# A two-block transformer on one core: closing a stage later, swapping two steps of a softmax pipeline on VectorE, and moving one weight load behind a wait

## What is computed

```python
q, k_cmp, v_cmp, ... = split(h @ w_in)            # 8 heads of 64, 2 key/value heads
for c in range(4):                                # 128 queries at a time
    s_c = q[c] @ k_cmp.T + head_bias(d_c)         # 31 compressed keys
    p_c = masked_softmax(s_c, d_c >= 0);  o_c = p_c @ v_cmp
    s_s = q[c] @ k_s.T + head_bias(d_s)           # selected keys
    p_s = masked_softmax(s_s, d_s >= 0);  o_s = p_s @ v_s
    s_w = q[c] @ k_w.T + head_bias(d_w)           # window of keys
    p_w = masked_softmax(s_w, m_w);       o_w = p_w @ v_w
    out[c] = g0 * o_c + g1 * o_s + g2 * o_w
mq, mk = silu(causal_conv(mq_mk) + b)             # for the mLSTM that follows
```

## Time and profile before

| | |
|---|---|
| median of 3 runs | 1873.73 us (1873.18 to 1878.88) |
| the profiled execution | 1878.88 us, span 1877.1 us |
| mean granted PE clock | 0.961 of full |
| busy over the span | PE 92%, PEld 66%, DVE 39%, ACT 32%, POOL 9% |
| chain that ended last | PE 69%, DMA 20%, DVE 5%, ACT 4% |
| DMA traffic | 341.73 MB, mean 182 GB/s |
| the stage of the change, "nsa" | from about 1088 to 1221 us |

### The profile page before, as it was taken

How to read it: one execution, slowest core, us unless ns; L and a number is a source line. 1 busy time by engine, 2 the same in 40 slices (tenths; PEclk the granted TensorE clock), 3 DMA queues, 4 the chain that set the end, 5 groups by cost and what they waited for, 6 DMA issues and landing times.

```text
span 1877.1 us, 22099 instructions
## 1 busy us (share of the span) xinstructions
PE 1726.2 (92%) x9084; PEld 1234.8 (66%) x9084; DVE 728.2 (39%) x1523; ACT 602.2 (32%) x1054; POOL 174.3 (9%) x132
## 2 busy tenths in 40 slices
PE   6999999997898888888889999998999999999998
PEld 5878767886333333333349877766787788888886
DVE  4355444455121111111125567654744442222223
ACT  3434354423010000000224446544624442222232
POOL 1000110231111111111001000011000000000221
PEclk9999999998899999899899999998999999999999
DMA  6512100358699999999984431011520222223201
GB/s 248 187 45 90 46 23 23 133 193 309 255 398 418 412 413 400 407 413 411 409 343 182 164 110 60 7 46 71 199 86 19 98 101 90 90 71 140 104 23 45
DMA packets 78994, 341.73 MB, mean 182 GB/s; under 512 B 7943, under 2 KB 15751, under 8 KB 65448
## 3 DMA queue, kind: packets, MB, share of 16 engines
q1 hardware_dynamic: 73768, 331.86, 45.7%
q0 software_dynamic: 5120, 8.40, 1.3%
HBM read 329.75 MB, written 18.87 MB: 186 GB/s over the span
## 4 chain that ended last, share of the span: by engine, by line
PE 69%; DMA 20%; DVE 5%; ACT 4%; issue 2%; SPq 0%; POOL 0%; DVEq 0%; POOLq 0%; ACTq 0%
PE ps L541 66%; DMA otf<-in_w 19%; PE ps L959 1%; PE ps L2785 1%; ACT splitr L617 1%; DMA ring<-in_w_in 1%; PE ps L794 1%; DVE arenaf L2867 1%; DVE splitr L606 0%; DVE arenaf L2885 0%; ACT arenaf L948 0%; DVE xf L3163 0%; DVE hr L848 0%; ACT hr L814 0%; ACT arenaf L855 0%
## 5 line engine op out<-in xcount | busy, mean ns | idle before, releaser
L541 PE MATMUL ps<-hr,splitr 128*128 128x512 f32 (+1 forms) x2784 | 579.5, 368 | 7.1 <-POOL hr L891 4.3
L541 PEld LDWEIGHTS ps<-hr,splitr 128*128 128x128 f32 x2784 | 476.9, 193 | 89.6 <-issue 5.3
L541 PE MATMUL ps<-splitr,hr 128*128 128x512 f32 (+1 forms) x1488 | 272.3, 343 | 2.2 <-DVE hr L1056 1.4
L541 PEld LDWEIGHTS ps<-splitr,hr 128*128 128x128 f32 x1488 | 234.6, 189 | 35.4 <-issue 1.9
L606 DVE TENSOR_TENSOR splitr<-ring,splitr 128x2048 fp32r<-128x2048 f32 x61 | 142.9, 2343 | 229.4 <-ACT splitr L617 229.4
L541 PE MATMUL ps<-ring,arenaf 128*64 128x512 f32 x352 | 170.7, 642 | 12.0 <-DMA ring<-in_w 12.0
L617 ACT CAST splitr<-ring 128x2048 fp32r<-128x2048 f32 x61 | 116.1, 1904 | 145.2 <-PE ps L541 140.0
L2010 DVE TENSOR_TENSOR arenaf<-arenaf,ps 64x512 f32<-64x512 f32 x32 | 21.8, 681 | 330.0 <-ACT arenaf L2005 330.0
L541 PE MATMUL ps<-arenaf 128*64 128x128 f32 (+9 forms) x754 | 110.5, 353 | 14.2 <-DVE arenaf L1835 6.0
L2005 ACT ACTIVATE arenaf<-ps 64x512 f32<-64x512 f32 x32 | 19.0, 595 | 311.7 <-PE ps L541 311.7
L541 PE MATMUL ps<-splitf,arenaf 128*64 128x512 f32 x320 | 87.1, 706 | 27.2 <-DMA splitf<-in_w 27.2
(11 more groups left out here) (381 smaller groups left out, 1920.7 us busy)
## 6 DMA issues: line engine op xcount, KB each, us to landing
ring<-in_w SPq DMA_DIRECT2D x22, 2048.0 KB, 36.1
arenaf<-in_w SPq DMA_DIRECT2D x22, 2048.0 KB
splitf<-in_w SPq DMA_DIRECT2D x21, 2048.0 KB, 35.1
hf<-in_w SPq DMA_DIRECT2D x20, 2048.0 KB, 36.4
ring<-in_w_in SPq DMA_DIRECT2D x11, 2048.0 KB, 12.5
otf<-in_w SPq DMA_DIRECT2D x11, 2048.0 KB, 40.2
ring<-in_w_gate_up SPq DMA_DIRECT2D x7, 2048.0 KB, 7.9
arenaf<-in_w_in SPq DMA_DIRECT2D x4, 2048.0 KB
```

Of the source, the lines that this page charges most:

```text
L541: return te.matmul(out, lhsT, rhs, start=start, stop=stop)
```

## The change

Four edits. The stage "nsa in" is closed for DVE after the first copy of `mcol`, and for ACT after the exponential of `mcol`; before, DVE closed it after the copies of `kCm` and ACT after its last Silu. The event of the compressed values and PE's wait for it go away, since the stage's end now covers them. In `ve_nsa` each step does N(s-1) and then B(s), where it did B(s) and then N(s-1). And in `sp_nsa` the load that follows `mqk` is issued behind the load of the biases of pair 2, and so behind the wait for the maximum of unit 8, and no more ahead of it; the load that follows `mv` keeps its place.

```diff
@@ ve_project_nsa
                                     *ve_done("vector copies", ("free", "cmp2", 0)))
-                        S.close("ve", "nsa in")
                     else:
                         for i in range(4):
                             ve.tensor_copy(vC4[96 - 32 * i:127 - 32 * i, :, i, :], thirds(ps[0:31, 0:128], 2)).then_inc(
-                                *ve_done("vector copies", ("compressed values",), ("free", "cmp2", 1)))
+                                *ve_done("vector copies", ("free", "cmp2", 1)))
...
                 ve.tensor_copy(mcol[:, 0, :, :], thirds(bank("mcol")[:, 0:16], 4)).then_inc(
                     *ve_done("vector copies", ("mcol0",), ("free", "mcol")))
+                S.close("ve", "nsa in")
@@ se_project_nsa
-                S.close("se", "nsa in")
                 for w in se_at(("mcol",), ("mcol0",)):
                     se.wait_ge(*w)
                 se.activation(mcol[:, 1, :, :], thirds(bank("mcol")[:, 16:32], 4), ACT.Exp).then_inc(
                     *se_done("powers", ("mcol1",), ("free", "mcol")))
+                S.close("se", "nsa in")
@@ pe_nsa
                         if br == 0:
-                            for w in pe_at(("compressed values",)):
-                                te.wait_ge(*w)
@@ ve_nsa
-                for part, u in nsa_steps(("B", "N", "beat", "E")):
+                for part, u in nsa_steps(("N", "B", "beat", "E")):
@@ sp_nsa
-                sp_used_jobs("mqk")
                 for p in (2, 3):
                     for w in sp_at(("max", "ns", 9 * (p - 2) + 8)):
                         sp.wait_ge(*w)
                     sp.dma_start(U[p % 2], Usrc[p]).then_inc(*sp_done(f"position biases {p % 2}", ("U", p), by=16))
-                sp_used_jobs("mv")
+                    sp_used_jobs(("mqk", "mv")[p - 2])
```

## The result

The changed kernel took 1898.21 us (median of 4 runs, 1890.9 to 1899.39) beside 1875.24 us of the kernel before (4 runs, 1873.18 to 1878.88). The ratio on record is 1.0106, with a 95% interval of 1.0088 to 1.0124: slower, by 16.5 to 23.3 us of 1875. It is not the quotient of these two medians (1.0122). Twenty-nine executions of the changed kernel are on record, from 1890.9 to 1902.09 us with a median of 1895.4, so the median of the four happens to lie high. The profiled execution took 1897.86 us, its span is 1896.1 us, 19.0 more than before.

The account below looks back on a forecast made before the run. PE was taken to bound the stage, busy 125.0 of 133 us. The terms 2.4 + 11.8 + 3.5 + 1.2 + 3.4 + 1.7 gave 24.0 us on the median 1873.7, so 1897.7 us; range 1884 to 1908.

Parts of the forecast that it names:

- PE's wait at the entry: Stage's entry: A(0) waits for ACT's exponential of mcol, +2.4 us, bounds 2.2 to 2.6.
- edits 2 and 3 up to C(10): N ahead of B on DVE and mv's load behind unit 8's maximum: C(10) at 1141.5 against 1129.68, +11.8 us; clock 1.7.
- ring, C(10) to C(19): B, exp and N of successive units in one chain take 37.0 us against 33.5 between these places, +3.5.
- ring, C(19) to C(28): The same chain plus ACT's four Silu and table loads: 33.8 us against 32.6, +1.2.
- ring, C(28) to C(35): The same chain through turns 30 to 35 and a weight piece: 24.5 us against 21.1, +3.4.
- the forecast's lower bound for the clock: Low clock after PE's stall before C(8): 1.7 us forecast, bounds 0 (the ring hides a slow PE) and 4.7.
- The ring's own share: Up to C(10) with the load hidden: C(10) at 1131.9, +2.2 us from the order of N and B.
- The rest of the ring: From C(10) to C(35): held banks wait for output copies behind B; 8.1 us together, bounds -4 and +14.
- The ring costs nothing: Rival: PE's slack absorbs DVE's lag everywhere, only load, entry and clock cost; +11.0 us, 1884.7 us, chance 0.15.
- The load is hidden: Rival: mv lands before ACT's cast matters, while the ring costs; +12.7 us, 1886.4 us, chance 0.12.
- Faster: Rival: N in DVE's idle time removes C's 7.5 us of waits and the load hides; 1868.6 us, chance 0.04.
- The clock stays low: Rival: low clock through small matmuls and transposes up to C(10), 4.7 us for 1.7; 1900.7 us, chance 0.15.

Follow-up runs that it names:

- entry alone: The kernel before with only the two `S.close(...)` lines moved and the event of the compressed values removed; ratio 1.0020, stage 138.30 us.
- order alone: The kernel before with N(u-1) ahead of B(u) on DVE and nothing else; ratio 1.0031, stage 141.24 us.
- load alone: The kernel before with the load of mv behind the maximum of unit 8 and nothing else; ratio 1.0045, stage 142.11 us.
- the two kernels that beat the one before: The kernel before with N(u-1) first only where DVE waits anyway, 0.9959; the same with a portion of mqk ahead of A(0), 0.9971.

## Why the prediction was right, and where its terms were off

The forecast was 1897.7 us and 24.0 us more; the runs gave 1898.21 (median of four) and some 20 more by the ratio, the stage 21.9. That 1897.7 comes within 1 us of the four is partly luck, since all 29 executions have a median of 1895.4. All three edits cost, by the mechanism named for each. The parts by places counted from the turning of mcol, forecast and measured:

| | forecast | changed kernel | alone |
|---|---|---|---|
| PE's wait at the entry | 2.4 | 2.5 | 2.5 |
| clock at the entry | not in the sum | 3.5 | 3.1 |
| edits 2 and 3 up to C(10), with the clock | 13.5 | 9.6 | 1.0 (order), 9.5 (load) |
| ring, C(10) to C(19) | 3.5 | 3.2 | 3.2 |
| ring, C(19) to C(28) | 1.2 | 0.4 | 0.4 |
| ring, C(28) to C(35) | 3.4 | 2.7 | 2.7 |
| clock behind C(35) | not in the sum | 0 | 1.3 (order) |
| stage | 24.0 | 21.9 | 23.7 |

- **Entry.** The wait was right to 0.1 us. The drain that the Trainium skill (ScalarE: Activation LUTs, "What ACT_TABLE_LOAD costs") adds to a table load doesn't show here either: the exponential starts 1.29 us behind the start of the load. What failed is that nothing was added for the clock, which cost 3.5 us. The rows used for it were of an idle time of 3.36 us. With the entry alone 2.59 us were enough; in the changed kernel the clock was down before the wait could count. By chance this omission of 3.5 is about what the next term had too much (3.9), so the total is better than its parts.
- **Up to C(10).** Forecast 11.8 + 1.7 = 13.5, measured 15.65 at C(10) less the 6.03 that the entry had cost at C(0): 9.6. The maximum of unit 8 was 2.4 us late beyond the entry, not 3.2 (2.4 with the order alone too); mv landed in 9.7 us, not 10.7; C(8) could do its first half before the stall, since only its second bank hangs on ACT's copy; and the low clock cost little in the changed kernel: 3.2 of its 10.2 us lay behind PE's start, and PE then waits 0.37 us for DVE's output copy, which comes right behind B(11), at the end of the ring. So the forecast's lower bound for the clock, 0 (the ring hides a slow PE), was close to right; in the run with the load alone, without the ring and with 6.1 us of the low clock behind PE's start, it cost 2.9. The forecast's "landed in 7.9 us alone" read the earlier trace rows too simply: another 2 MB went out 0.42 us behind that load (1086.44). The number holds all the same, 7.9 us in the run with the load alone, where nothing followed. The ring's own share, 1.0 us, was forecast with 2.2.
- **The rest of the ring.** The mechanism and the places hold (a ring of B, exp and N, pinned at the output copies), and the sizes nearly. C(19) to C(28) was put too high: while ACT's two table loads and the Silu ran (1182.73 to 1188.40) PE stood for nothing, and its first wait behind C(19) ends at 1194.62, 0.79 us long.
- **Rivals.** "The ring costs nothing" is refuted by the order alone, +8.6 us, 7.3 of it without the clock. "The load is hidden" is refuted by the load alone, +9.5. "Faster" is refuted for N first everywhere; its reason, that N can use DVE's idle time, is true of the steps behind a beat, and shows in the two kernels that beat the one before. "The clock stays low" came true for its length (10.2 us in the changed kernel and with the load alone), not for its price there.
- **Behind the stage** nothing changed beyond what profiles of one kernel differ by: 657.2 us before, 656.0 after.

Of the three edits in the stage the load is the dearest alone (9.5 us), the order next (8.6), the entry last (5.7, of which 2.5 is the wait). Together they cost 1.8 us less than apart, but 1.3 of that is the fall of the clock at the end of the order's profile: up to C(35) the three come to 22.4 apart and 21.9 together, so they all but add up.

## What to carry to other kernels

Which of two steps goes first on an engine isn't a matter of the sum of its work: write down what each waits for and what runs beside it. Putting the normalization first is right where the engine waits for scores anyway, and wrong where it takes away the overlap with another engine's exponentials; a mixed order can win where either pure one doesn't. A load's place in an issuing queue is to be judged by the first engine that stands at its landing in program order, and by all that engine has queued behind, not by when the data are multiplied; and a wait of 2 to 3 us on PE is to be priced with the clock that may be low behind it, 1.3 to 3.5 us here in the profiles that show a fall. Before a difference of a few us between two profiles is explained, compare the clock in both.

## What the runs showed of the hardware that had not been expected

- The clock was at 1.2 GHz behind an idle time of PE of only 2.6 us in six of six kernels, for 6.8 us (five) or 10.2 us (one), and dense work there took 4.25 to 5.5 us for 3.06. In three of the six it fell 0.1 to 0.4 us after PE had started again; in the other three it fell 0.1 to 0.3 us after PE's last small transposes, ahead of nearly all of the idle time. It fell in the same way in one kernel of eight without that wait (5.49 us for 3.02), right behind narrow products and small transposes. The rule of the Trainium skill (TensorE: Matmul & The Clock Gate, "PE-mode transpose") that transposes don't count as work for the gate fits these four early falls, but they don't decide it: the narrow products are a cause as likely.
- In the three long stalls before the second half of C(8) (8.38, 7.00 and 6.53 us) the clock fell 1.3, 0.9 and 2.4 us after PE's last work, and stayed down for 10.2 us each time.
- A shorter wait may or may not come with a fall: PE waits 2.2 us before C(35) in seven profiles, and in four of them the clock fell there for 3.4 us (1.3 to 1.6 us lost), in three, the changed kernel's among them, it didn't.
- Two executions of the same first work of the stage can differ by 3.1 us through the clock alone (1.73 + 5.49 us against 1.08 + 3.02), so gains of that size need the clock of each profile beside them.
- A 2 MB load landed in 7.9 and 8.1 us alone, 8.8 with 0.9 MB issued right behind it (but 7.9 in the kernel before with another 2 MB right behind it), and in 9.7 to 10.9 us in four kernels with the same 0.9 MB ahead of it.
